# Mixing norm's root taken behind its projections, its squares summed during the down projection, and weight splits put in front of the roots of three stages

## The chip, the cores and the metric

The kernel runs on one core of one Trainium2 chip. The metric is the device time of one execution in microseconds (us). The kernel before takes 2094.03 us (median of three executions, 2090.93 to 2095.31).

## What is computed

Two transformer blocks run one after the other over 512 tokens of width 1024 in fp32. The change touches the second block, whose sequence has 16 meta tokens in front (528 tokens). Of it this matters:

```python
def rmsnorm(x, g):
    y = xf * lax.rsqrt(jnp.mean(xf * xf, axis=-1, keepdims=True) + EPS)
    return y * g
h = h + 0.5 * swiglu(rmsnorm(h, ffn1_norm), w_gate, w_up, w_down)      # stages up2, down2
u = rmsnorm(h, mix_norm)                                              # the mixing norm
(aq, ak, av, gq, gk, gv, gr, g_low, gate_a, gate_b) = split(u @ w_in) # stage back
ya = window_sink_attention(aq, ak, av, sinks)
log_a = log_sigmoid(g_low @ gla_gate_w + gla_gate_b) / 16
og = gated_linear_attention(gq, gk, gv, log_a)
yb = rmsnorm(og, gla_out_norm) * silu(gr)
mixed = sigmoid(gate_a) * (ya @ w_branch_att) + sigmoid(gate_b) * (yb @ w_branch_gla)  # merge2
h = h + mixed @ w_out                                                 # out2
h = h + 0.5 * swiglu(rmsnorm(h, ffn2_norm), ...)                      # up3, down3
```

The root of a token is one number that multiplies the whole row of `u`. So `u @ w_in` equals `(h * g) @ w_in` times that number, and the factor can be put on the product.

## The kernel before

Activations lie with features on the 128 partitions: eight tiles `k` of 128 features by 528 tokens. Each fp32 operand of a projection is split into a high and a low part (`H_hi`/`H_lo`, `W_hi`/`W_lo`, `G_hi`/`G_lo`), and TensorE forms hi·hi, lo·hi and hi·lo, three matmuls for each pair of tiles. Weights come in chunks of 128x2048 (`WC`; down projections 128x1408; the first chunk of `back`, "low", 128x1024). There are two buffers of each kind. SyncE loads chunk c into `W_raw` when chunk c-2 is split; ScalarE's `split` copies it to `W_hi` when TensorE has used chunk c-2; VectorE's `split` makes `W_lo` from both; TensorE then uses the chunk. ScalarE, VectorE and TensorE each run their instructions strictly in the order of the code, so what stands ahead of a `split` there delays it. The matmuls of a chunk have two groups of PSUM banks in turn (`psum_free0`, `psum_free1`), and a group is used again when an engine has evicted it.

The stages that matter come in this order: `up2` (22 chunks), `down2` (16 chunks, two for each feature tile of the residual `X`), `back` (14 chunks), `merge2` (8), `out2` (4), `up3` (22), `down3`.

- The norms ahead of `up2` and `up3` (`RMS_1`, `RMS_2`) are "late": TensorE starts with `H = x * gain`, and inside the second chunk it sums the squares over the partitions (`late_root`, in `project_late`). ScalarE takes the square root, VectorE the reciprocal into `RS`, and VectorE multiplies each product by `RS` as it evicts it (line 2089). `walk(..., after_first=...)` sets the order on ScalarE and VectorE: split of the second chunk, root, eviction of the first chunk, split of the third chunk.
- The mixing norm (`RMS_MIX`) is a plain one. After the last tile of `down2`, TensorE sums eight squared tiles (`statistic`), ScalarE takes the root, VectorE the reciprocal `INV`, then for each tile VectorE scales, ScalarE rounds to `H_hi`, and VectorE makes `H_lo`. The chunk "low" of `back` follows the tiles one by one, and the split of the next chunk stands behind all of them.
- `back` begins with four chunks in a row: "low" (16 columns, which go into the small gate matmuls), two of queries, one of keys and values. Then `win_steps` (35 steps of the windowed attention, each with some six projection matmul groups between) and `gla_steps` (30 steps of the gated linear attention) are woven with the remaining ten chunks. ScalarE and VectorE run the same steps in the same order. Products are evicted by ScalarE in the main (`back_low`, `back_query`, `back_key_value`, `back_value`, `back_gate`).

## Time and profile before

| | |
|---|---|
| median of three executions | 2094.03 us (2090.93 to 2095.31) |
| profiled execution, its own time | 2093.15 us |
| its span, from first to last instruction | 2091.3 us |
| TensorE (PE) busy | 1983.7 us, 95% |
| VectorE (DVE) busy | 1005.7 us, 48% |
| ScalarE (ACT) busy | 727.0 us, 35% |
| mean granted TensorE clock | 0.983 of full speed |

TensorE is the engine that is nearly always at work; a time to its left in the rows further down is in us from the start of the span. "PE PS L600" is any matmul (line 600 is the helper that issues them), "DVE W_lo L1625" is VectorE's split, "ACT ... L1184" any operation of ScalarE.

### The profile page before, as it was taken

What the parts mean: (1) busy time and instruction counts of PE and PEld (TensorE: products, weight loads), DVE (VectorE), ACT (ScalarE), POOL (GpSimd) and SP (SyncE); (2) the same over time, 40 slices, a digit from 0 to 9 for tenths busy, and PEclk for the clock granted to TensorE, in tenths of its full rate; (3) what the DMA queues carried; (4) which work ended last, traced back from release to release, by engine and by line L of the source; (5) the groups of instructions that cost most, each with busy time, mean ns of one, the idle gap of its engine ahead of it and who ended that gap; (6) DMA issues with size and microseconds to landing.
All of it is one profiled execution on the core that took longest, in us unless ns stands there. A gap on an engine that the chain in (4) does not pass through costs nothing.

```text
span 2091.3 us, 26797 instructions
## 1 busy us (share of the span) xinstructions
PE 1983.7 (95%) x10909; PEld 1671.3 (80%) x10909; DVE 1005.7 (48%) x1364; ACT 727.0 (35%) x972; POOL 23.8 (1%) x45
## 2 busy tenths in 40 slices
PE   5899999997999999979999999899999999999997
PEld 2787887873888888769999999687888878888885
DVE  7688753436455542264443322667323454444323
ACT  2454444324445532152222212455333332222111
POOL 0100000000000000000000000000000000000000
PEclk9999999998999999999999999999999999999999
DMA  6644212220222222212222222211112222222221
GB/s 269 215 158 134 99 61 102 102 99 20 81 97 83 100 83 97 102 39 82 100 80 94 72 95 92 73 61 42 61 61 81 102 81 99 100 100 74 97 90 61
DMA packets 34847, 195.45 MB, mean 93 GB/s; under 512 B 3680, under 2 KB 3696, under 8 KB 19552
## 3 DMA queue, kind: packets, MB, share of 16 engines
q1 hardware_dynamic: 29008, 173.55, 23.6%
q0 software_dynamic: 5776, 21.02, 3.1%
q8 instruction: 44, 0.72, 0.1%
q14 instruction: 19, 0.16, 0.0%
HBM read 192.46 MB, written 2.10 MB: 93 GB/s over the span
## 4 chain that ended last, share of the span: by engine, by line
PE 88%; DVE 8%; ACT 2%; issue 1%; DMA 1%; SPq 0%; DVEq 0%; ACTq 0%
PE PS L600 86%; DVE W_lo L1625 2%; DVE INV L1669 1%; DMA A_low<-in_wada 1%; PE PS L756 1%; ACT W_hi L1184 1%; DVE N L1674 1%; DVE A_high L2103 1%; DMA ring<-in_wada 0%; DVE ring L2103 0%; DVE RS L1646 0%; DVE PT_lo L1707 0%; DVE stats L1692 0%; DVE X L2135 0%; DVE stats L1856 0%
## 5 line engine op out<-in xcount | busy, mean ns | idle before, releaser
L600 PE MATMUL PS<-H_hi,W_hi 128*128 128x512 f32 (+1 forms) x1976 | 632.2, 354 | 48.8 <-DVE H_lo L1657 19.4
L600 PE MATMUL PS<-H_hi,W_lo 128*128 128x512 f32 (+1 forms) x1976 | 632.9, 354 | 0.0
L600 PE MATMUL PS<-H_lo,W_hi 128*128 128x512 f32 (+1 forms) x1976 | 632.0, 354 | 0.0
L1625 DVE TENSOR_TENSOR W_lo<-W_raw,W_hi 128x2048 fp32r<-128x2048 f32 (+2 forms) x170 | 352.9, 2076 | 311.6 <-ACT W_hi L1184 311.0
L600 PEld LDWEIGHTS PS<-H_hi,W_hi 128*128 128x128 f32 x1976 | 350.0, 191 | 106.6 <-issue 42.8
L1184 ACT ACTIVATE W_hi<-W_raw 128x2048 fp32r<-128x2048 f32 (+2 forms) x170 | 295.6, 1739 | 325.4 <-PE PS L600 324.6
L600 PEld LDWEIGHTS PS<-H_lo,W_hi 128*128 128x128 f32 x1976 | 349.3, 191 | 50.6 <-issue 0.2
L600 PEld LDWEIGHTS PS<-H_hi,W_lo 128*128 128x128 f32 x1976 | 349.1, 191 | 49.9 <-issue 0.2
L600 PE MATMUL PS<-G_hi,W_lo 128*128 128x512 f32 (+1 forms) x704 | 210.2, 339 | 0.0
L600 PE MATMUL PS<-G_hi,W_hi 128*128 128x512 f32 (+1 forms) x704 | 209.6, 338 | 0.0
L600 PE MATMUL PS<-G_lo,W_hi 128*128 128x512 f32 (+1 forms) x704 | 209.3, 338 | 0.0
L2089 DVE TENSOR_TENSOR T<-PS,RS 128x528 f32<-128x528 f32 (+1 forms) x88 | 57.4, 694 | 174.5 <-PE PS L600 174.4
L600 PEld LDWEIGHTS PS<-G_lo,W_hi 128*128 128x128 f32 x704 | 120.6, 188 | 15.7
L600 PEld LDWEIGHTS PS<-G_hi,W_hi 128*128 128x128 f32 x704 | 120.6, 188 | 15.2 <-issue 0.4
L600 PEld LDWEIGHTS PS<-G_hi,W_lo 128*128 128x128 f32 x704 | 120.4, 188 | 15.3
L1184 ACT ACTIVATE G_hi<-T 128x1024 f32 (+3 forms) x33 | 35.3, 1070 | 231.8 <-DVE T L2095 210.7
L2061 DVE SCALAR_TENSOR_TENSOR T<-PS,V,T 128x511 f32<-128x511 f32 (+1 forms) x88 | 60.0, 744 | 111.4 <-ACT T L1184 111.4
L1184 ACT ACTIVATE T<-T 128x1024 f32<-128x1024 f32 (+1 forms) x34 | 36.4, 1070 | 155.5 <-DVE T L2089 154.5
L1184 ACT ACT_TABLE_LOAD x45 | 57.7, 1283 | 51.5 <-PE PS L600 50.2
L1184 ACT ACTIVATE PT_hi<-PS 128x128 fp32r<-128x128 f32 (+3 forms) x64 | 27.9, 437 | 100.2 <-PE PS L756 100.2
L600 PE MATMUL PS<-W_lo,H_hi 128*128 128x256 f32 x208 | 62.0, 298 | 0.0
L600 PE MATMUL PS<-W_hi,H_hi 128*128 128x256 f32 x208 | 59.4, 286 | 2.1 <-DVE W_lo L1625 2.1
(246 smaller groups left out, 2045.2 us busy)
## 6 DMA issues: line engine op xcount, KB each, us to landing
W_raw<-in_wts SPq DMA_DIRECT2D x119, 1024.0 KB, 4.8
W_raw<-in_wdown SPq DMA_DIRECT2D x48, 704.0 KB, 4.1
ring<-in_wada POOLq DMA_DIRECT2D x32, 512.0 KB, 3.8
A_high<-in_wada SPq DMA_DIRECT2D x6, 1024.0 KB, 18.0
A_low<-in_wada SPq DMA_DIRECT2D x2, 1024.0 KB, 10.5
X<-in_xT SPq DMA_DIRECT2D x2, 1024.0 KB, 10.0
X<-in_xT POOLq DMA_DIRECT2D x1, 2048.0 KB, 8.8
out<-N SPq DMA_DIRECT2D x8, 256.0 KB, 2.1
```

The lines of the kernel that those rows point to most:

```text
L600: return nc.tensor.matmul(*a, **kw)
L756: last = nc.tensor.transpose(PS[:, TURNED, j * P:(j + 1) * P], PR[:, u % 3, j * P:(j + 1) * P], ident)
L1184: return nc.scalar.activation(*a, **kw)
L1625: vector.tensor_tensor(W_lo[:, c.odd, 0:size], W_raw[:, c.odd, 0:size], W_hi[:, c.odd, 0:size].bitcast(FP32), ALU.subtract).then_inc(w_lo, 1)
L1669: vector.reciprocal(INV[:, 0:n.tok], DEV[:, 0:n.tok]).then_inc(n.sem("inverse"), 1)
L1674: vector.scalar_tensor_tensor(out=N2[:, k, 0:n.tok], in0=n.centred(k), scalar=n.gain(k), in1=INV[:, 0:n.tok], op0=ALU.mult, op1=ALU.mult). ...
L2061: ins = vector.scalar_tensor_tensor(out=tile[:, m, tap:SEQ], in0=PS[:, 4 * b.odd + 2 * m, 0:SEQ - tap], scalar=w, in1=tile[:, m, tap:SEQ], ...
L2089: ins = vector.tensor_tensor(halves((TA, TB)[k][:, m, 0:tok], tok), pview(b, m, tok), halves(RS[:, 0:tok], tok), ALU.mult)
L2103: vector.scalar_tensor_tensor(out=w, in0=w, scalar=1.0, in1=silu_c[:, :], op0=ALU.mult, op1=ALU.mult, accum_out=mod[:, t:t + 1]).then_inc( ...
```

## The change

Five things are done; the rest of the diff is what they need (buffers, semaphores).

1. `down2` is written out tile by tile on ScalarE and VectorE. As soon as a residual tile is there, ScalarE makes `H_hi = x * gain` and the square, and VectorE makes `H_lo` and adds the square to a running sum in `TA`. The split of `back`'s second chunk (the first queries) stands right behind the last tile.
2. TensorE starts "low" without a norm, and sums `TA` over the partitions inside the first query chunk, after three of its eight tiles (`late_root`). The small gate matmuls behind that chunk wait for ScalarE's root. 16 matmuls of statistics go, 2 come.
3. All products of `back` are multiplied by the root. VectorE does it as it evicts low, queries, keys and values, the `gr` and gate chunks (before, ScalarE evicted these). The factors of the linear attention's q and k are multiplied by `RS` in three operations at attention steps 3 to 5 (`back_factor`). For the token-major values TensorE turns `RS` into a column of 5 numbers for each partition (5 matmuls of one column), VectorE copies it (`RSC`), and ScalarE scales with it, in four operations in place of two. In `merge2` VectorE multiplies the gate product and ScalarE then takes its sigmoid from SBUF.
4. In `up2` and `up3` (and in `back` on ScalarE) the split of the third chunk stands ahead of the root on ScalarE, and ahead of the reciprocal on VectorE.
5. In `up3` TensorE sums the squares after two tiles of the second chunk, not after six.

```diff
-                chunks_of_round(0, 0, s.words[0])
+                split(At(s.c + 1), s.words[0])
+                after_first()
+                for k in range(per):
+                    body(0, 0, k)
...
-            pool.wait_ge(*RMS_MIX.reach("scaled", 1))
+            pool.wait_ge(w_used, st["back"].c)
+            pool.wait_ge(sem("hidden_lo"), 2 * FH)
...
+                        n = 6 if tok == TOK else 2
+                        feature_tile(outs_of(b, m, tok, at), c.odd, 0, tiles * P, range(n), act_hi, act_lo, stop=False)
                         within_first()
-                        feature_tile(outs_of(b, m, tok, at), c.odd, 6 * tiles * P, tiles * P, range(6, KT), act_hi, act_lo, start=False)
+                        feature_tile(outs_of(b, m, tok, at), c.odd, n * tiles * P, tiles * P, range(n, KT), act_hi, act_lo, start=False)
...
+            def late_root(n):
+                pe.wait_ge(*n.reach("added", n.sums))
+                total = TA if n is RMS_MIX else N1
+                for o, (t0, tn) in n.outs(n.late_bank):
+                    last = mm(o, inv_d[:, :], total[:, 0, t0:t0 + tn], start=True, stop=True)
...
+                        for n in range(NB + 1):
+                            t0 = META + n * P if n < NB else 0
+                            mm(PS[:, TURNED, 2 * P + n:2 * P + n + 1], RS[:, t0:t0 + P], ident[:, 0:1], start=True, stop=True)
...
+                            if k == 1 and m == 0 and kt == 3:
+                                late_root(RMS_MIX)
...
+                        pe.wait_ge(*RMS_MIX.reach("deviation", 1))
...
-            norm(RMS_MIX, st["back"].held)
...
+            def square_of(k):
+                n = RMS_MIX
+                wait_src(act, n, k)
+                if k == 0:
+                    act.wait_ge(sem("hidden_prod"), HIDDEN["up2"] + FH + 1)
+                if k >= 4:
+                    act.wait_ge(*n.reach("added", k - 3))
+                activate(square_tile(k), n.src(k), ACT.Square).then_inc(n.sem("squared"), 1)
...
+            def back_query(g):
+                act.wait_ge(sem("att_q_raw"), g + 1)
+                activate(WQH[:, 2 * g:2 * g + 2, :], GR[:, 2 * g:2 * g + 2, :], ACT.Copy, scale=QSCALE).then_inc(sem("att_q_hi"), 1)
...
+            def back_key():
+                act.wait_ge(sem("att_k_raw"), 1)
                 for at, tok, n in KEY_PIECES:
-                    ins = activate(KWH[:, at:at + n], PS[:, back_bank(b, tok // HALF), tok % HALF:tok % HALF + n], ACT.Copy)
+                    ins = activate(KWH[:, at:at + n], KT_flat[:, tok:tok + n], ACT.Copy)
...
-                for m in range(2):
-                    ins = activate(LV[:, 2 * m:2 * m + 2, col:col + 256], PS[:, bank + m, :].rearrange("p (b n) -> p b n", b=2), ACT.Copy)
+                for blk in range(NB):
+                    ins = activate(LV[:, blk, col:col + 256], PS[:, bank + blk // 2, blk % 2 * 256:blk % 2 * 256 + 256], ACT.Copy,
+                                   scale=RSC[:, blk:blk + 1])
...
                 split(At(s.c + 2), words[s.c + 2])
+                late_root(RMS_MIX)
                 back_logit()
-                back_query(s, 1)
+                back_query(0)
...
+                    split(At(s.c + 2), WC)
...
-            only_split("down2", 4, 4)
-            norm(RMS_MIX)
+            s = st["down2"]
+            for f in range(KT):
+                for half in range(2):
+                    split(At(s.c + 2 * f + half + 1), words[s.c + 2 * f + half + 1])
+                    if f and half == 0:
+                        late_tile(RMS_MIX, f - 1)
+                        square_of(f - 1)
+            late_tile(RMS_MIX, KT - 1)
+            split(At(st["back"].c + 1), WC)
+            square_of(KT - 1)
...
+            def add_square(k):
+                n = RMS_MIX
+                dve.wait_ge(*n.reach("squared", k + 1))
+                if k >= 2:
+                    dve.wait_ge(*n.reach("added", k - 1))
+                vector.tensor_tensor(square_tile(0), square_tile(0), square_tile(k), ALU.add).then_inc(n.sem("added"), 1)
+            def mix_root():
+                n = RMS_MIX
+                add_square(KT - 1)
+                dve.wait_ge(*n.reach("deviation", 1))
+                vector.reciprocal(RS[:, :], RS[:, :]).then_inc(n.sem("inverse"), 1)
                 dve.wait_ge(*n.reach("inverse", 1))
...
+            def back_low(s):
+                used(At(s.c))
+                retire(vector.tensor_tensor(halves(TC[0:RANK, 0, :], TOK), PS[0:RANK, 0:2, 0:HALF], halves(RS[0:RANK, :], TOK), ALU.mult),
+                       s, At(0))
+            def scaled_pair(s, k, dst, done):
+                used(At(s.c + k))
+                b, g = BATCH_OF[k], BACK[k][1]
+                bank = back_bank(b, 0)
+                vector.tensor_tensor(dst[:, 2 * g:2 * g + 2, :], PS[:, bank:bank + 2, :], root_twice(), ALU.mult).then_inc(sem(done), 1)
+            def freed(k, done, value):
+                dve.wait_ge(sem(done), value)
+                dve.sem_inc(psum_free[BATCH_OF[k] % 2], 1)
...
+                dve.wait_ge(sem("back_part"), PART_OF[k])
+                vector.tensor_tensor(halves(KT_flat, TOK), back_halves(b), halves(RS[:, :], TOK), ALU.mult).then_inc(sem("att_k_raw"), 1)
+                freed(k, "att_k_raw", 1)
+                used(At(s.c + k))
+                vector.tensor_tensor(halves(VT[:, :], TOK), back_halves(b + 1), halves(RS[:, :], TOK), ALU.mult).then_inc(sem("att_v"), 1)
+                dve.wait_ge(sem("att_v"), 1)
+                dve.sem_inc(psum_free[(b + 1) % 2], 1)
                 dve.wait_ge(sem("att_k_hi"), 1)
                 for at, tok, n in KEY_PIECES:
-                    ins = vector.tensor_tensor(KWL[:, at:at + n], PS[:, back_bank(b, tok // HALF), tok % HALF:tok % HALF + n],
...
+            def back_factor(n):
+                dve.wait_ge(sem("decays"), 1)
+                to, of = ((TA, LE), (TB, TB), (LL, LL))[n]
+                vector.tensor_tensor(to[:, :, :], of[:, :, :], root_all(), ALU.mult).then_inc(sem("factors"), 1)
...
+                    if 3 <= t < 6:
+                        back_factor(t - 3)
...
+                    if k > BACK_FIRST_GLA:
+                        scaled_gate(s, k - 1)
+                yield GLA_STEPS
+                scaled_gate(s, len(BACK) - 1)
+            def scaled_gate(s, k):
+                what, g, _ = BACK[k]
+                dst, done = (GR, "gr_raw") if what == "gr" else (GB, "gate_kept")
+                scaled_pair(s, k, dst, done)
+                freed(k, done, g + 1)
...
             def back(s):
-                split(At(s.c + 1), words[s.c + 1])
+                mix_root()
+                back_low(s)
                 split(At(s.c + 2), words[s.c + 2])
+                scaled_pair(s, 1, GR, "att_q_raw")
+                freed(1, "att_q_raw", 1)
                 back_abs()
-                back_query(s, 1)
+                back_query(0)
                 split(At(s.c + 3), words[s.c + 3])
                 back_sums()
-                back_query(s, 2)
+                scaled_pair(s, 2, GR, "att_q_raw")
+                freed(2, "att_q_raw", 2)
+                back_query(1)
...
+                        if name == "merge2":
+                            used(c)
+                            for m in range(2):
+                                ins = vector.tensor_tensor(TB[:, m, 0:SEQ], PS[:, 4 * b.odd + 2 * m, :], RS[:, META:TOK], ALU.mult)
+                            retire(ins, s, b)
...
+                walk(dve, split, s, FH, 2, body, lambda: late_root(n, lambda: split(At(s.c + 2), WC)))
...
-            residual_sum("down2", 1, 0.5, TOK, 0)
-            norm(RMS_MIX)
+            s = st["down2"]
+            for f in range(KT):
+                b = At(f)
+                for half in range(2):
+                    split(At(s.c + 2 * f + half + 1), words[s.c + 2 * f + half + 1])
+                used(At(s.c + 2 * f + 1))
+                x = halves(X[:, f, :], TOK)
+                vector.scalar_tensor_tensor(out=x, in0=pview(b, 0, TOK), scalar=0.5, in1=x, op0=ALU.mult, op1=ALU.add
+                                            ).then_inc(sem("residual"), 1)
+                dve.wait_ge(sem("residual"), RESIDUAL["down2"] + f + 1)
+                dve.sem_inc(psum_free[f % 2], 1)
+                late_tile(RMS_MIX, f)
+                if f >= 2:
+                    add_square(f - 1)
+            split(At(st["back"].c + 1), WC)
```

How the instructions stand is seen at three places.

VectorE around the root of `up2`, before (`N1` or `N` are the squares, `T` the evicted product, `W_lo` a split):

```order
L1643 TENSOR_TENSOR N<-N 128x1056 x3
L1643 TENSOR_TENSOR N<-N 128x528
L1646 RECIPROCAL RS<-RS 128x528
L2089 TENSOR_TENSOR T<-PS,RS 128x528 x2
L1625 TENSOR_TENSOR W_lo<-W_raw,W_hi 128x2048
L2089 TENSOR_TENSOR T<-PS,RS 128x528 x2
```

The same place in the changed kernel:

```order
L1683 TENSOR_TENSOR N<-N 128x528
L1665 TENSOR_TENSOR W_lo<-W_raw,W_hi 128x2048
L1687 RECIPROCAL RS<-RS 128x528
L2193 TENSOR_TENSOR T<-PS,RS 128x528 x4
L2199 TENSOR_TENSOR T<-T 128x1056
```

The split of the third chunk has moved from behind the reciprocal and the first eviction to ahead of both. `up3` shows the same with 128x512.

VectorE from the last down split to the splits of `back`, before (`X` the residual, `INV` and `N` the norm, the 128x1024 split is "low"):

```order
L1625 TENSOR_TENSOR W_lo<-W_raw,W_hi 128x1024
L2036 SCALAR_TENSOR_TENSOR X<-PS,X 128x528
L1669 RECIPROCAL INV<-DEV 128x528
L1674 SCALAR_TENSOR_TENSOR N<-X,V,INV 128x528 x2
L1655 TENSOR_TENSOR H_lo<-N,H_hi 128x528
...
L1655 TENSOR_TENSOR H_lo<-N,H_hi 128x528 x2
L1625 TENSOR_TENSOR W_lo<-W_raw,W_hi 128x2048 x2
```

The same place in the changed kernel (`T<-T` adds a square to the sum, `T<-PS,RS 16x528` evicts "low", `GR` takes the first queries):

```order
L1665 TENSOR_TENSOR W_lo<-W_raw,W_hi 128x1024
L2318 SCALAR_TENSOR_TENSOR X<-PS,X 128x528
L1673 SCALAR_TENSOR_TENSOR H_lo<-X,V,H_hi 128x528
L1695 TENSOR_TENSOR T<-T 128x528
L1665 TENSOR_TENSOR W_lo<-W_raw,W_hi 128x2048
L1695 TENSOR_TENSOR T<-T 128x528
L1701 RECIPROCAL RS<-RS 128x528
L1835 TENSOR_TENSOR T<-PS,RS 16x528
L1665 TENSOR_TENSOR W_lo<-W_raw,W_hi 128x2048
L1843 TENSOR_TENSOR GR<-PS,RS 128x1024
```

The reciprocal now stands behind the split of the first query chunk and ahead of the split of the second; sixteen operations of the norm (scale and low part of eight tiles) have gone from between.

VectorE in the attention's steps 2 to 4 in the changed kernel (`stats` and `PRW` are the softmax of one unit, `PTW_lo` and `PTM_lo` the low part of its turned probabilities):

```order
L1665 TENSOR_TENSOR W_lo<-W_raw,W_hi 128x2048
L1885 TENSOR_TENSOR T<-LE,RS 128x1056
L1939 TENSOR_REDUCE stats<-PS 128x1
L1942 TENSOR_SCALAR stats<-stats,V 128x1
L1949 TENSOR_TENSOR stats<-stats 128x1
L1952 RECIPROCAL stats<-stats 128x1
L1954 TENSOR_SCALAR PRW<-PRW,stats 128x272
L1962 TENSOR_TENSOR PTW_lo<-PS,PTW_hi 128x128
L1964 TENSOR_TENSOR PTM_lo<-PS,PTM_hi 16x128
L1885 TENSOR_TENSOR T<-T,RS 128x1056
```

The two rows with `RS` are new, and a third (`LL<-LL,RS`) follows one step later; without them the rows are those of before.

## Rows read from the trace of the kernel before

**Rows 1.** Page: busy us by engine; one group: xcount | busy us, mean ns | idle

```profile
PE 1983.7 (95%) x10909; PEld 1671.3 (80%) x10909; DVE 1005.7 (48%) x1364; ACT 727.0 (35%) x972; POOL 23.8 (1%) x45
...
L2089 DVE TENSOR_TENSOR T<-PS,RS 128x528 f32<-128x528 f32 (+1 forms) x88 | 57.4, 694 | 174.5 <-PE PS L600 174.4
```

**Rows 2.** Waits of PE over the span: total us, times, longest us

```profile
PE PS L600 <- DVE W_lo L1625: 12.0, 4, 3.8
PE PS L600 <- DVE H_lo L1655: 7.5, 4, 6.6
```

**Rows 3.** Timeline, end of down2 and start of back: start, us, what [idle before]

```profile
1301.24 0.41 PE L600 MATMUL PS<-G_hi,W_lo 128*128 128x264 f32 x2
...
1302.56 7.36 PE L600 MATMUL PS<-SQ,inv_d 128*128 128x264 f32 x32 [0.91 <-issue]
...
1303.09 1.28 ACT L1184 ACT_TABLE_LOAD   x1
...
1316.51 0.78 PE L600 MATMUL PS<-H_hi,W_hi 128*128 128x264 f32 x2 [6.59 <-DVE H_lo L1655]
...
1324.11 1.90 ACT L1184 ACTIVATE W_hi<-W_raw 128x2048 fp32r<-128x2048 f32 x1
...
1328.39 0.50 PE L600 MATMUL PS<-H_hi,W_hi 128*128 128x512 f32 x1 [2.39 <-DVE W_lo L1625]
```

**Rows 4.** Timeline, first query chunk's end to the attention's first steps

```profile
1339.72 2.04 PE L600 MATMUL PS<-T 16*128 16x264 f32 x8
...
1346.29 2.29 DVE L1625 TENSOR_TENSOR W_lo<-W_raw,W_hi 128x2048 fp32r<-128x2048 f32 x1
...
1350.74 1.26 DVE L1815 TENSOR_TENSOR T<-T 128x1056 f32<-128x1056 f32 x1 [2.16 <-ACT T L1184]
...
1355.86 1.22 DVE L1781 SCALAR_TENSOR_TENSOR WQL<-PS,WQH 128x1024 fp32r<-128x1024 f32 x1
...
1361.18 1.06 DVE L1791 TENSOR_TENSOR KWL<-PS,KWH 128x264 fp32r<-128x264 f32 x6 [1.66 <-ACT KWH L1184]
...
1375.12 0.40 PE L600 MATMUL PS<-KWH,WQH 64*128 64x272 f32 x2 [1.44 <-ACT PRW L1184]
...
1376.02 0.44 DVE L1856 TENSOR_REDUCE stats<-PS 128x1 f32<-128x272 f32 x1 [0.52 <-PE PS L600]
```

**Rows 5.** Timeline of PE, the linear attention's first turns and its end

```profile
1472.48 1.28 PE L894 MATMUL PS<-CF,LL 128*128 128x128 f32 x10
...
1565.05 0.49 PE L600 MATMUL PS<-H_hi,W_hi 128*128 128x512 f32 x1 [1.39 <-ACT GB L1184]
```

**Rows 6.** Timeline, root of up2 and of up3

```profile
925.01 1.05 PE L600 MATMUL PS<-N,inv_d 128*128 128x264 f32 x4
925.71 0.60 PE L600 MATMUL PS<-H_hi,W_hi 128*128 128x264 f32 x2
...
926.84 3.45 DVE L1646 RECIPROCAL RS<-RS 128x528 f32<-128x528 f32 x1 [2.69 <-ACT RS L1184]
...
937.03 0.51 PE L600 MATMUL PS<-H_hi,W_hi 128*128 128x264 f32 x2 [3.66 <-DVE W_lo L1625]
...
1712.11 1.02 PE L600 MATMUL PS<-N,inv_d 128*128 128x512 f32 x2
...
1723.91 0.79 PE L600 MATMUL PS<-H_hi,W_hi 128*128 128x512 f32 x1 [3.82 <-DVE W_lo L1625]
```

**Rows 7.** Windows: span, length, busy us (instructions) by engine, granted clock, DMA share, GB/s

```profile
937.00:942.00 5.00, 4.97 (x28) 4.98 (x29) 3.64 (x4) 2.55 (x2) 0.00 (x0) 0.66 0.60 211
1326.00:1330.00 4.00, 1.61 (x8) 1.34 (x8) 3.82 (x2) 2.41 (x3) 0.00 (x0) 1.00 0.20 37
1365.00:1463.00 98.00, 88.92 (x708) 78.02 (x707) 71.12 (x243) 51.51 (x182) 0.00 (x0) 0.98 0.13 44
1419.00:1422.00 3.00, 3.00 (x17) 2.50 (x17) 2.16 (x6) 0.39 (x3) 0.00 (x0) 0.52 0.24 44
1724.00:1730.00 6.00, 6.00 (x15) 4.70 (x16) 4.27 (x5) 2.86 (x2) 0.00 (x0) 0.52 0.49 175
```

More of the change, by code:

```diff
@@ L190, in build_program @@
         one = sb("one", [P, 1], FP32)
+        RSC = sb("RSC", [P, NB + 1], FP32)
         small = sb("small", [P, 3, GLA_HEADS * NB], FP32)
@@ L1088, in merge_one @@
                         last.then_inc(w_used, 1)
-            def late_root(n):
-                pe.wait_ge(*n.reach("added", 4))
-                for o, (t0, tn) in n.outs(n.late_bank):
-                    last = mm(o, inv_d[:, :], N1[:, 0, t0:t0 + tn], start=True, stop=True)
-                last.then_inc(n.sem("variance"), 1)
             def project_late(name, n, norm_of, tok, at):
```

110 lines of the change are left out of this document (53 added, 57 removed).

## The prediction

> **What bounds the kernel now.** I read the page's busy times first: TensorE is busy for 1983.7 us of the span, VectorE for less than half [rows 1]. So time is won only where TensorE stops or runs at a lower clock. The waits of TensorE say for whom it stops: 12.0 us for splits, with the longest 3.8 us, and 7.5 us for the low parts that the mixing norm makes [rows 2]. The timeline then shows what lies around three of these stops, and the windows the clock behind them.
>
> - *End of `down2`.* The last down matmul pair is issued at 1301.24. A query chunk's 48 matmuls of 512 columns take 11.33 us (1328.39 to 1339.72), 0.236 us each, so a pair of 264 columns takes 0.243, and the next chunk could start at 1301.49. The first query chunk really starts at 1328.39 [rows 3, 4]. In these 26.9 us TensorE does statistics (7.36 us), waits 6.59 us for the first normed tile, does "low" at the pace of the norm, and waits 2.39 us for the split [rows 3].
> - *Roots of `up2` and `up3`.* TensorE waits 3.66 and 3.82 us for the split of the third chunk, which on both other engines stands behind root, reciprocal and first eviction [rows 6]. Behind each wait the granted clock falls to its lower level, 1.2 GHz: its mean is 0.66 over the 5 us from 937, and 0.52 over the 6 us from 1724 [rows 7]. Behind the wait of 2.39 us at 1328.39 it stays at 1.00, which is 2.4 GHz [rows 3, 7].
>
> **What the parts of the change cost and give.** All is reckoned against the profiled execution's own 2093.15 us, which is 0.9 us under the median of the runs; its span is 2091.3 us, and the 1.8 us around it stay.
>
> *The gap behind `down2`.* What remains of the 26.9 us is "low": 24 pairs at 0.243 us, 5.9 us with the start. It may run at once, since seven of eight tiles are made during `down2`, and the last comes in time: three operations on 528 columns (residual, `H_hi`, `H_lo`) at some 0.7 us, the mean of that size [rows 1], from 1301.7 to 1304.0, and TensorE gets to it at about 1306.7. The split of the query chunk: `W_hi` 1.90 us behind `H_hi` (1303.2 to 1305.1), `W_lo` 2.29 us, so 1307.4, just as "low" ends [rows 3, 4]. TensorE then starts queries at 1307.45 in place of 1328.39. **Gain 20.9 us.** In `down2` each engine gets two such operations more per tile. A chunk there is 33 pairs, 8.0 us of TensorE; a split behind residual, tile and sum is done 5 us into it (0.7 of 2048 columns' 1.90 and 2.29 for the split, and 2.1), so they cost nothing. Without that cover they would cost 1.4 us a tile, 11 in all.
>
> *The root in the query chunk.* Two matmuls of sums delay TensorE by 0.7 us (925.01 to 925.71 is the same) [rows 6]. **Cost 0.7 us.** The chunk's matmuls take 11.3 us, so it ends at 1319.45. ScalarE: `W_hi` of the next chunk from 1307.5 to 1309.4, table load 1.28, root 0.7, so 1311.4. VectorE: reciprocal 3.45, low 0.6, split 2.29, so 1317.8 [rows 1, 3, 4, 6]. TensorE wants this split only after the gate matmuls, 2.04 us [rows 4], at 1321.5. Margin 3.7 us, no wait.
>
> *Up to the attention.* Query chunk two runs to 1332.8. VectorE evicts the first queries (1.22 us, by the row for 1024 columns from PSUM), and the rest goes as before; the split for the key chunk is ready at 1328.4 [rows 4]. The gate sums on VectorE take 5.1 us (1350.74 to 1355.86) from 1330.6 to 1335.8, then queries two 1.2 us; the value half needs that group only at 1338.7. But what follows is late: low part of the queries, the split (2.29, to 1342.3), keys times root (0.7, to 1343.0) [rows 1, 4]. ScalarE's decays end at 1344.3, then the key's high part 0.8; TensorE has finished the value half at 1344.5. VectorE still has values times root (0.7) and the key's low part (1.06 for six pieces, 0.9 for five) [rows 4], so 1346.1. Before, that part was done in the middle of the chunk. Queued behind it are the first scores, and with them all of TensorE. **Cost 1.7 us**, between nothing (if the chain runs ahead) and 2.2.
>
> *In the attention.* Five one-column matmuls are ten passes; ten turns of 128 columns take 1.28 us at most [rows 5]. **Cost 1.1 us.** Three products with `RS` of 1056 columns cost VectorE 1.26 us each [rows 4], the copy of `RSC` 0.2. They stand ahead of the row maximum, for which ScalarE's exponential and TensorE's next scores wait. There TensorE already stops 1.44 us on this chain, so the first counts in full, while VectorE was idle 0.52 us before the next maximum [rows 4] and I give the third about as much. **Cost 2.8 us**, bounds 0 (all in idle time) and 4.0 (all on the path). Scaling the values in four operations instead of two lengthens ScalarE's step twice by some tenths. No row shows the 256-column form; it costs between nothing and one wait like 1.44 us, and I take 0.3.
>
> *Behind it.* Gate evictions move from ScalarE to VectorE, 1.2 us in place of 1.0; only the last is waited for, as now with 1.39 us [rows 5]. **Cost 0.2 us.** In `merge2` the product comes 11 us ahead of its use: nothing. Without that cover 1.3 us for each of four.
>
> *`up2` and `up3`.* The split of the third chunk fits between the sums and the root: in `up2` VectorE's sums end before TensorE takes them, at 925.01, in fact at 924.2; ScalarE has nothing between the first chunk's end and the root, and `W_lo` is done at 926.5; the reciprocal starts at 926.84 as it does now [rows 6]. TensorE's second chunk ends at 933.4, when the first is long evicted. In `up3` the sums come 2.8 us earlier (1709.3), which makes room: the split ends at 1712.3, the reciprocal follows to 1715.7, the eviction to 1717, and TensorE is there at 1720. Both stops go, with the clock that they cost: 5 x 0.34 = 1.7 us and 6 x 0.48 = 2.9 us [rows 7]. **Gains 3.7 + 1.7 and 3.8 + 2.9 us**, 12.1 in all.
>
> Sum: 20.9 + 12.1 - 0.7 - 1.7 - 1.1 - 2.8 - 0.3 - 0.2 = 26.2 us, so 2093.15 - 26.2 = **2067.0 us**, 1.3% faster.
>
> **The rivals.**
>
> - *The root comes too late (a new wait in the place of the old).* The chain root, reciprocal, low, split is serial, and the margin of 3.7 us is my reckoning. If it slips by more, TensorE stops ahead of the second query chunk, and with a stop as long as those of `up2` the clock falls behind it: 3.7 + 1.7, so 2072.4. Against it: each link has a row. Chance 0.13.
> - *The attention hides it all.* VectorE is busy 71.1 of 98 us there [rows 7]. If the factors and the key chain fall into its idle time, the costs 1.7 and 2.8 go: 2062.5. Against it: TensorE already waits in these steps. Chance 0.15.
> - *The clock falls once more.* The stop ahead of the first scores and those of the next steps lie close together. One fall like that behind `up2` or `up3` adds 1.7 to 2.9 us: 2069.5. Chance 0.12.
> - *The stops of `up2` and `up3` only move* to the next chunk, if its PSUM group is still taken: 12.1 us are not won, 2079. Against it: eviction ends 1.7 and 3 us before need. Chance 0.06.
> - *Slower: the attention at the low clock.* There TensorE does small groups between waits. At 1419 the clock fell to 0.52 for some 3 us although TensorE was at work [rows 7]. If the added stops keep it at 1.2 GHz, each us at that level loses about 0.48 us (from the 6 us at 0.52). The gain of 26.2 us is used up when 55 of the 98 us run so; over the whole stage the loss is 47 us and more, and the time 2115. The Trainium skill ("TensorE: Matmul & The Clock Gate", section "A second HAM failure mode: psum-queue depth-cycling") speaks for this: TensorE that idles briefly but often between matmul groups has its clock go down and up again, and throughput suffers. By that rule, the trace agrees only in part: this stage already has such idle moments and its mean clock is 0.98. Chance 0.04.
>
> **How the numbers follow.** My own forecast holds 0.50, the rivals the rest. From 2062 to 2074.5 lie my forecast with its bounds (-4.5 if the attention hides all, +1.2 and +0.5 for factors and keys at their upper ends, +1.2 for the values), most of the second rival, the first and the third: about 0.83. Within 0.2% (4.2 us, about what a measurement of this kernel can tell from no change) would take a loss of 22 us out of the sum: 0.02. Slower 0.04, faster 0.94.
>
> **What the profile of the changed kernel would show.** Right: no matmul on `SQ` at the end of `down2`, "low" at once and at full clock, its last pair followed by the queries within 0.5 us; no stop of TensorE over 1 us at either third chunk of `up2` and `up3`, and clock 1.00 behind; a stop of 1 to 2.5 us ahead of the first scores, released by `KWL`; TensorE's idle time in the attention up by about 3 us. Wrong: a wait for `W_lo` ahead of the second query chunk; a wait for an eviction (`T<-PS,RS`) in `up2` or `up3`; splits of `down2` that TensorE waits for; a mean clock under 0.95 in the attention.

## The result, and the profile after

The changed kernel takes 2077.76 us (median of four executions, 2077.51 to 2079.00) against 2093.36 us before beside it (median of four; 2090.93 to 2095.31); the ratio is 0.9928, with a 95% interval of 0.9914 to 0.9941. It is faster, by 15.6 us where 26.2 were forecast, and lies outside the forecast range of 2062 to 2074.5 us. The profiled execution of after took 2077.65 us, with a span of 2075.8 us.

The first lines of the page of after, which answer to [rows 1] (share of the span and instructions behind each busy time):

```profile
span 2075.8 us, 26753 instructions
PE 1982.6 (96%) x10891; PEld 1667.3 (80%) x10891; DVE 1025.1 (49%) x1385; ACT 723.9 (35%) x965; POOL 23.8 (1%) x45
```

The waits of TensorE of after (total us, times, longest), which answer to [rows 2]:

```profile
PE PS L621 <- ACT PRW L1212: 4.0, 2, 2.6
PE PS L913 <- DVE PTM_lo L1964: 2.5, 3, 2.1
PE PS L621 <- DVE PTM_lo L1964: 2.5, 4, 0.9
PE PS L621 <- DVE W_lo L1665: 2.1, 1, 2.1
PE PS L621 <- DVEq L1847: 1.6, 1, 1.6
```

Of the 12.0 us for `W_lo` one wait of 2.1 us in the first block is left, and the 7.5 us for `H_lo` of the mixing norm are gone. `ACT PRW`, the probabilities that the next scores wait for, rose to 4.0 from this row of before:

```profile
PE PS L600 <- ACT PRW L1184: 2.8, 2, 1.4
```

The timeline of after behind `down2` answers to [rows 3]. The row with `G` is the last pair of `down2`; the first row of TensorE (PE) with 128x512 is the first of the queries:

```profile
1300.32 0.41 PE L621 MATMUL PS<-G_hi,W_lo 128*128 128x264 f32 x2
1300.77 0.71 DVE L2318 SCALAR_TENSOR_TENSOR X<-PS,X 128x528 f32<-128x528 f32 x1 [5.65 <-PE PS L621]
1301.51 0.74 ACT L1212 ACTIVATE H_hi<-X,V 128x528 fp32r<-128x528 f32 x1 [7.65 <-DVE X L2318]
1302.16 1.90 ACT L1212 ACTIVATE W_hi<-W_raw 128x2048 fp32r<-128x2048 f32 x1
1304.09 2.29 DVE L1665 TENSOR_TENSOR W_lo<-W_raw,W_hi 128x2048 fp32r<-128x2048 f32 x1 [0.42 <-ACT W_hi L1212]
1306.44 0.50 PE L621 MATMUL PS<-H_hi,W_hi 128*128 128x512 f32 x1
1308.63 1.05 PE L621 MATMUL PS<-T,inv_d 128*128 128x264 f32 x4
1310.66 3.45 DVE L1701 RECIPROCAL RS<-RS 128x528 f32<-128x528 f32 x1 [3.66 <-ACT RS L1212]
1318.66 2.04 PE L621 MATMUL PS<-T 16*128 16x264 f32 x8
1320.63 0.50 PE L621 MATMUL PS<-H_hi,W_hi 128*128 128x512 f32 x1
```

From the last matmul pair of `down2` to the first query matmul it is 6.12 us, where it was 27.15: a gain of 21.03. No row of TensorE here has a wait in brackets, at the second query chunk (1320.63) neither.

The windows of after (the columns are busy us and instructions of PE, PEld, DVE, ACT and POOL, then the granted clock), for `up2` behind its third chunk, and for `up3`, which answer to [rows 7]:

```profile
930.00:948.00 18.00, 18.00 (x150) 18.00 (x149) 10.90 (x8) 5.98 (x5) 0.00 (x0) 1.00 0.24 80
1700.00:1725.00 25.00, 25.00 (x108) 20.08 (x107) 14.17 (x11) 9.72 (x9) 0.00 (x0) 1.00 0.24 85
```

TensorE is busy without a gap and at 2.4 GHz: both stops are gone, with the low clock behind them [rows 6, 7].

The attention of after, with the new costs in it. The scores (`KWH,WQH`) stop TensorE for 2.01 us, and a factor product (`T<-LE,RS`, 1.24 us) stands ahead of the chain on which the next scores wait for 2.62 us, with its brackets `<-ACT PRW`:

```profile
1345.76 0.34 PE L621 MATMUL PS<-KWH,WQH 64*128 64x144 f32 x2 [2.01 <-issue]
1352.72 0.40 PE L621 MATMUL PS<-KWH,WQH 64*128 64x272 f32 x2 [0.35 <-DVE RSC L1877]
1357.42 1.24 DVE L1885 TENSOR_TENSOR T<-LE,RS 128x1056 f32<-128x1056 f32 x1
1359.93 0.59 PE L621 MATMUL PS<-KWH,WQH 64*128 64x272 f32 x2 [2.62 <-ACT PRW L1212]
```

So where are the missing us? The first and last start of the matmuls on one tile give the length of each stretch. The table has them in us, worked out from those starts in each trace (experiments beside it):

| stretch | before | after | e1 | e4 | e5 | e10 | e13 |
|---|---|---|---|---|---|---|---|
| merge1 (first matmul on O to first on M) | 77.0 | 78.2 | 77.0 | 77.0 | 76.2 | 76.3 | 76.3 |
| out1 (M, first to last) | 43.3 | 44.6 | 43.2 | 43.2 | 43.3 | 43.3 | 43.3 |
| norms and up1, to first on G | 295.2 | 294.9 | 294.0 | 295.2 | 290.0 | 289.7 | 289.4 |
| down1 (G) | 122.1 | 122.8 | 122.2 | 122.1 | 123.1 | 120.0 | 119.9 |
| norm and up2 | 291.0 | 286.7 | 285.5 | 284.2 | 284.6 | 284.4 | 284.4 |
| down2 | 127.8 | 128.3 | 127.8 | 127.8 | 127.8 | 127.8 | 127.8 |
| back, and merge2 to first on O2A | 274.9 | 263.8 | 262.5 | 274.9 | 264.5 | 267.9 | 261.5 |
| merge2, to first on M2 | 77.0 | 78.1 | 77.0 | 77.0 | 77.0 | 77.0 | 76.9 |
| out2 (M2) | 43.2 | 44.6 | 43.2 | 43.2 | 43.2 | 43.3 | 43.3 |
| up3 | 252.6 | 245.7 | 245.8 | 245.8 | 240.5 | 240.5 | 240.5 |
| down3 | 121.8 | 122.6 | 121.9 | 121.9 | 120.7 | 119.4 | 119.5 |

Stages in which TensorE has the same work as before got longer: merge1 by 1.2 us, out1 by 1.3, down1, down2 and down3 by 0.5 to 0.8, merge2 by 1.1, out2 by 1.4, which is 7.0 us in all. The change rewrote `down2` and the evictions of `merge2` on the other two engines, but it left the first block alone, and each matmul takes longer there too. What changed in all of them is the place of the buffers: `CB` (512 bytes in each partition) went into an overlay and `RSC` took 32 bytes, so what is allocated behind `RSC`, among it O, M and G, lies 480 bytes lower. The weights `W_hi` and `W_lo` and the activations H are allocated ahead of both and stayed.

### The profile page after: what moved, and what is told of

It is laid out like the page before. It is cut to its first block, busy times and chain, and to the rows that moved or that the text cites. A ratio compares the mean times of both kernels' runs of the same rounds, so it can differ in the third digit from the quotient of the medians.

```text
span 2075.8 us, 26753 instructions
## 1 busy us (share of the span) xinstructions
PE 1982.6 (96%) x10891; PEld 1667.3 (80%) x10891; DVE 1025.1 (49%) x1385; ACT 723.9 (35%) x965; POOL 23.8 (1%) x45
## 4 chain that ended last, share of the span: by engine, by line
PE 89%; DVE 7%; ACT 1%; issue 1%; DMA 1%; SPq 0%; DVEq 0%; ACTq 0%
PE PS L621 88%; DVE W_lo L1665 1%; DMA A_low<-in_wada 1%; PE PS L778 1%; DVE INV L1724 1%; DVE A_high L2207 1%; DMA ring<-in_wada 0%; DVE ring L2207 0%; ACT W_hi L1212 0%; DVE N L1729 0%; DVE PT_lo L1762 0%; DVE stats L1747 0%; DVE X L2239 0%; DVE stats L1939 0%; DVE PTW_lo L1962 0%
## 5 line engine op out<-in xcount | busy, mean ns | idle before, releaser
L1212 ACT ACTIVATE T<-T 128x1024 f32<-128x1024 f32 (+1 forms) x38 | 40.6, 1069 | 171.6 <-DVE T L2193 149.4
```

What stands on the lines that cost most here:

```text
L1212: return nc.scalar.activation(*a, **kw)
```

## The experiments

**The place of the buffers (e1, e2, e3) and the roots alone (e4).** e1 is the changed kernel with

```diff
-        one = sb("one", [P, 1], FP32)
-        RSC = sb("RSC", [P, NB + 1], FP32)
+        ones = sb("ones", [P, 1 + NB + 1], FP32)
+        one, RSC = ones[:, 0:1], ones[:, 1:NB + 2]
```

e2 is the kernel before with `sb("pad", [P, 8], FP32)` ahead of `mod`; e3 the kernel before with `CB` in its overlay and `sb("pad", [P, 16], FP32)` in its old place; e4 the kernel before with parts 4 and 5 of the change, in `up2` and `up3` alone.

> The changed kernel, with RSC put into the 32 bytes that `one` has in each partition anyway, so that every buffer behind it lies at a multiple of 128 bytes again where it did before (512 bytes lower), not 32 bytes past one. Theory A (the address): in the changed kernel the matmuls of 512 columns that read M, O, O2A and O2G take 395 ns in place of 389 (0.2333 us from one to the next in out2 in place of 0.2267), 768 of them, 5.1 us, and the 1056 wide ones on G about 1 ns each more. So here 389 ns again, the part up to up2 shorter by 2.8 us, merge2 and out2 by 2.5, the time 2077.8 - 5.5 = 2072 us. Rival B (the cadence differs from run to run, or comes from VectorE's traffic in merge2): 395 ns stays, 2077.8 us.

> The kernel before, with nothing but an unused buffer of 32 bytes per partition ahead of `mod`, so that all that lies behind it starts 32 bytes later. Theory A (the address): M, O, O2A, O2G at 395 ns, 5 to 6 us slower than before, 2099 us, half of it ahead of up2. Rival B (the cadence has nothing to do with the address): no change, 2093.4 us.

> The kernel before, with CB in its overlay (as in the changed kernel) and an unused buffer of 64 bytes in its place: all that lies behind starts 448 bytes lower, at 64 bytes past a multiple of 128. It tells what alignment counts. Theory A1 (multiples of 64 bytes are enough): 389 ns, no change, 2093.4 us. Theory A2 (multiples of 128 are needed): 395 ns or more for M, O, O2A, O2G, 5 us slower, 2098.5 us. What speaks for A2: G's tiles are 2112 bytes apart and so lie at 0 and 64 past a multiple of 128 in turn, and their wide matmuls take 393 ns in the kernel before. Rival B (not the address): 2093.4.

> The kernel before, with the parts 4 and 5 of the change alone (split of the third chunk ahead of root and reciprocal in up2 and up3, sums after two tiles in up3); no address changes. By the prediction 12.1 us less, 2081.3 us. By what the trace of after shows (up2 and down2 together 3.8 us shorter where 5.4 were reckoned, merge2 to the final norm 3.6 where 6.7 were reckoned less 0.2, of which the address would explain 2.5): 9.8 us, 2083.6 us. Rival (the stops only move, or the clock falls elsewhere): 2088 us or more.

Measured, beside the kernel before (2093.43 us); four or five executions each, ten of e3: e1 2068.78 us (ratio 0.9886, 0.9870 to 0.9901); e2 2103.18 (1.0054, 1.0040 to 1.0068); e3 2097.68 (1.0018, 1.0009 to 1.0028); e4 2081.86 (0.9943, 0.9930 to 0.9957). The matmuls on M, one row of each trace (shortest, median and longest ns), in the order before, after, e1, e2, e3:

```profile
L600 PE MATMUL PS<-M_hi,W_hi x128: 389/389/389, 422.0 to 1696.1; 128*128 128x512 f32 x128
```
```profile
L621 PE MATMUL PS<-M_hi,W_hi x128: 393/395/397, 423.1 to 1686.4; 128*128 128x512 f32 x128
```
```profile
L621 PE MATMUL PS<-M_hi,W_hi x128: 389/389/389, 423.0 to 1678.0; 128*128 128x512 f32 x128
```
```profile
L601 PE MATMUL PS<-M_hi,W_hi x128: 393/395/397, 421.4 to 1704.8; 128*128 128x512 f32 x128
```
```profile
L601 PE MATMUL PS<-M_hi,W_hi x128: 397/397/398, 422.6 to 1702.7; 128*128 128x512 f32 x128
```

An unused pad of 32 bytes alone makes the kernel before 9.7 us slower; 32 bytes taken back make the changed kernel 9.0 us faster. Theory A stands, B falls. e3 shows that a multiple of 64 bytes isn't enough (A2). In e2 the stages named above account for 6.9 us, and between after and e1 they account for 6.9 us too. The rest of e2 lies in `up2` (2.1) and `back` (2.6), less `up3` (-1.1), and the first two go with the clock: H didn't move, and e2's trace has a mean granted clock of 0.97 in `up2` and 0.97 in the 270 us behind `down2`, where that of before has 0.98 in both (for `back` see the table of steps further down). So 7 us are shown to come from the address. Whether the other 2 to 3 us of e1 and e2 have to do with it isn't shown.

**What the distance must be (e5, e9, e10).** e5 views H and G as dense tiles wherever 512 tokens are used:

```diff
+        def dense_view(t, n):
+            return t[:, :, :].rearrange("p k t -> p (k t)")[:, 0:n * SEQ].rearrange("p (k t) -> p k t", t=SEQ)
+        HC_hi, HC_lo = dense_view(H_hi, KT), dense_view(H_lo, KT)
+        def g_of(tok):
+            return (G_hi, G_lo) if tok == TOK else (dense_view(G_hi, FT), dense_view(G_lo, FT))
```

> The changed kernel with RSC beside `one` (as in e1_aligned, 2068.8 us), and besides: where only 512 of the 528 tokens are used (all of the first block, up3, down1, down3), the tiles of H and G lie 2048 bytes apart and begin at a multiple of 128 bytes; till now they are 2112 apart, so every second one lies 64 bytes past a multiple. Theory A (the address of the moving operand costs): some 2900 matmuls of 512 columns on H and 1056 on G get faster; at half of the 8 ns that M lost between 0 and 64 bytes past (389 to 397 ns in e3_moved_64) that is 4 ns x 3960 = 16 us, 2053 us, and G goes from 393 to 389 ns. Rival B (it counts for M, O and O2 only, through what else runs there): no change, 2068.8 us.

> e1_aligned, and behind the final norm's sums 26 groups of 48 matmuls of 128x128 (24 to a PSUM bank; the last three groups 264 columns wide), ahead of them one group of 120. Their results are used nowhere. Stationary operand: four blocks of W_lo in turn; moving: W_hi, both at 128 bytes past a multiple of 512. The moving operand is shifted by 0, 16, 32, 64, 96, 128, 192, 224, 256, 288, 320, 384 and 448 bytes; then the stationary one by 32, 64, 128, 256 and 384; then both together by 64, 128 and 256; then every third moving operand alone by 384 and by 64. Theory A1 (64 bytes): 0.2267 us from one to the next at 0, 64, 128 ..., 0.2333 at 16, 32, 96, 224, 288. Theory A3 (512 bytes, or the distance between the two operands): 0.2267 at shift 0 alone; if it is the distance, also where both are shifted. e3_moved_64 speaks against A1 (M at 64 bytes past: 0.2333). Rival B (what else runs beside TensorE sets it): all groups alike.

> e5_dense (2057.1 us), with the dense tiles of G_lo begun 128 bytes later, so that they too lie at 128 bytes past a multiple of 512, as G_hi, H, M, O and the weights do. In e5_dense down1 took 123.1 us and down3 120.7 (122.2 and 121.9 in e1_aligned), and G_lo (at a multiple of 512) was the slower operand. Theory A3 (all operands at the same place in 512 bytes are fast): 0.2267 us per matmul in both, 528 of them, 119.7 us each, 2057.1 - 3.4 - 1.0 = 2052.7 us. Theory A1 (128 bytes are enough): no change, 2057.1 us.

e5 took 2057.14 us (0.9827, 0.9813 to 0.9841), 11.6 less than e1 where some 16 were expected, and e10 2054.34 (0.9812, 0.9798 to 0.9825), 2.8 less than e5 where 4.4 were expected. In the traces the two down stages did lose 4.4 us from e5 to e10; `back`, which they have in common, was 3.4 us longer in e10's. Against e1 the stretch of `up1` won 4.0 us and that of `up3` 5.3, but down1 got slower by 0.9. The probe tells why. Four of its 26 groups, from the trace of e9 (L1214: no shift; L1229: moving operand shifted by 128 bytes; L1238: by 256; L1271: both operands by 128):

```profile
L1214 PE MATMUL PS<-W_hi,W_lo x48: 389/389/389, 2085.0 to 2095.7; 128*128 128x512 f32 x48
L1229 PE MATMUL PS<-W_hi,W_lo x48: 392/394/398, 2140.4 to 2151.4; 128*128 128x512 f32 x48
L1238 PE MATMUL PS<-W_hi,W_lo x48: 389/389/397, 2174.0 to 2184.7; 128*128 128x512 f32 x48
L1271 PE MATMUL PS<-W_hi,W_lo x48: 387/389/398, 2296.0 to 2306.7; 128*128 128x512 f32 x48
```

From a group's first start to that of the next it is 10.9 us at no shift and at 256 bytes, 11.0 at 64 and 320, 11.1 at 16, and 11.2 at 32, 96, 128, 192, 224, 288, 384 and 448. Shifting the stationary operand alone does the same (11.2 us at 32, 64, 128 and 384, 10.9 at 256), and shifting both together costs nothing (10.9 at 64, 128 and 256). With every third moving operand alone off it is 11.0 at 384 bytes and 11.1 at 64. So neither A1 nor A3 was right as written: it is the distance between the two operands that counts, and it should be a multiple of 256 bytes. The other engines were idle by then, so rival B falls for good. The probe was executed once, and it doesn't repeat the kernel at 64 bytes: there a shift by 64 costs a third of one by 32 (11.0 and 11.2 us), while in e3, with M 64 bytes off, out2 takes the same 44.6 us as with M 32 bytes off (e2). So the multiple of 256 is shown, and what a given other distance costs is not settled. In e5 `G_lo` was 128 bytes off such a multiple. With that mended (e10), all wide matmuls on G take 389 ns:

```profile
L632 PE MATMUL PS<-G_hi,W_hi 128*128 128x512 f32 x352 | 137.0, 389 | 0.2 <-DVE G_lo L2196 0.2
L632 PE MATMUL PS<-G_hi,W_lo 128*128 128x512 f32 x352 | 136.9, 389 | 0.0
L632 PE MATMUL PS<-G_lo,W_hi 128*128 128x512 f32 x352 | 136.9, 389 | 0.0
```

and down1 and down3 fall to 120.0 and 119.4 us (expected 119.7). In e5 the trace leaves one thing unexplained: down3 ran faster than down1 with the same addresses.

**The terms of the attention (e6, e7, e8, e12), each against e1 (2068.78 us, 0.9886).** e6 leaves out the three calls of `back_factor`; e8 leaves out the five matmuls on `RS`, `RSC` and the `scale=`; e12 moves those matmuls ahead of the first scores; e7:

```diff
 # ScalarE
-                back_decays()
                 back_key()
+                back_decays()
 # VectorE
+                back_key(3)               # keys times RS, ahead of the split
                 split(At(s.c + 4), words[s.c + 4])
                 back_key_value(s, 3)      # KWL, and only then values times RS
```

> e1_aligned without the three products of back_factor: the linear attention's q and k are left without the root (this part of the computation is left out). The prediction counted 2.8 us for them: 2066.0 us. Theory C (they set off further stops or a fall of the clock, and so make up the missing us of the attention): 4 us or more, 2064.8 or less. Rival D (they lie in VectorE's idle time): 2068.8 us, no change.

> e1_aligned with the keys ahead in both queues: VectorE multiplies the keys ahead of the split of the fifth chunk and makes KWL ahead of the values; ScalarE makes KWH ahead of the decays. The prediction counted 1.7 us for the stop ahead of the first scores (2.01 us in the trace). If it goes and nothing takes its place: 2066.8 us. Theory C (the stop also sets off later ones and a lower clock): 2065.5 or less. Rival D (the stop goes, but the values or the decays are then late by as much): 2068.8 us.

> e1_aligned without the turned root: no matmuls of one column, no RSC, the token-major values are evicted unscaled in two operations in place of four (this scaling is left out). The prediction counted 1.1 us for the matmuls and 0.3 for the evictions: 2067.4 us. Theory C (they delay the chain of the scores and cost more): 2066 or less. Rival D (hidden): 2068.8 us.

> e1_aligned, with the five matmuls that turn the root put into TensorE's stop ahead of the first scores (2.01 us; they take 1.17). Leaving them and the scaled evictions out won 3.1 us (e8_no_turn, 2065.7), where the prediction counted 1.4. If the matmuls themselves cost (1.17 us and what they push back on the chain of the scores): 2067 us or less, down to 2066. Rival (the four evictions in place of two cost): 2068.8 us, no change.

Measured: e6 2064.55 us (0.9857, 0.9842 to 0.9872), 4.2 less than e1; e7 2067.26 (0.9868, 0.9853 to 0.9883), 1.5 less; e8 2065.72 (0.9866, 0.9851 to 0.9881), 3.1 less; e12 2066.41 (0.9866, 0.9851 to 0.9881), 2.4 less. These differences are small against what surrounds them. The intervals of all four touch that of e1, and e1 wasn't run beside them: by the ratios the same four differences are 6.1, 3.8, 4.2 and 4.2 us. So the traces have to tell what a term costs in its place.

Every second step of the attention starts with a group of scores on TensorE. The table has the time in us from the last matmul pair of `down2` to the first scores, and then the length of some of the stretches from one group of scores to the next, numbered from 1 to 15; those left out agree within 0.3 us. A star marks a stretch with a mean granted clock under 0.85 of full speed.

| stretch | before | e2 | after | e1 | e6 | e7 | e8 | e12 | e10 | e13 | e14 |
|---|---|---|---|---|---|---|---|---|---|---|---|
| to the first scores | 63.5 | 63.5 | 45.4 | 45.4 | 45.5 | 43.3 | 45.5 | 45.5 | 45.4 | 45.5 | 44.4 |
| 1 | 4.3 | 4.3 | 7.0* | 5.5 | 5.5 | 5.5 | 4.3 | 4.4 | 8.3* | 5.7* | 4.4 |
| 2 | 6.0 | 6.0 | 7.2 | 7.2 | 6.0 | 7.2 | 7.2 | 7.2 | 7.7* | 7.2 | 7.2 |
| 3 | 6.9 | 6.9 | 8.5* | 8.5* | 6.9 | 8.4* | 8.4* | 8.4* | 8.4 | 7.4 | 8.4* |
| 4 | 4.8 | 4.8 | 4.8 | 4.8 | 4.8 | 4.8 | 4.8 | 4.8 | 6.0* | 4.8 | 4.8 |
| 6 | 4.5 | 5.8* | 4.5 | 4.5 | 4.5 | 5.8* | 4.5 | 5.8* | 5.8* | 4.5 | 5.8* |
| 8 | 4.8 | 6.0* | 6.0* | 6.0* | 6.0* | 6.0* | 4.8 | 6.0* | 6.0* | 6.0* | 6.0* |
| 10 | 5.5* | 5.7* | 5.7* | 4.5 | 5.7* | 5.7* | 5.5* | 5.7* | 5.7* | 5.7* | 5.7* |
| 15 | 9.3 | 9.3 | 9.3 | 10.8* | 9.3 | 9.3 | 9.3 | 9.3 | 9.3 | 9.3 | 9.3 |

At equal clock the terms can be read off:

- *Keys (e7).* The first scores come 2.1 us sooner than in e1.
- *One-column matmuls (e8, e12).* Stretch 1 is 1.1 us shorter without them. With them in the stop, it is 1.05 us shorter, and the first scores come no later: the stop fell from 2.0 us to the row below. The copy of `RSC` and what goes with it is the 0.07 us between 4.33 us (e8) and 4.40 us (e12).
- *Factors (e6).* Stretch 2, with one product in it, is 1.2 us shorter without; stretch 3, with two, 1.5 us (8.4 at full clock in e10, 6.9 in e6). With only one product in it (e13) it is 7.4.
- *The clock.* From stretch 4 on the traces differ by 1.0 to 1.5 us at a time, and the star goes with the longer time, not the edit: stretch 8 takes 4.8 us in before and 6.0 in e2, which have the same attention. In stretch 3 the low clock costs nothing (8.4 us in e10 without it). e1 has three starred stretches, e6 and e8 two, e7 and e12 four. That is why the times don't measure the terms: of the 3.1 us of e8, 1.1 are the matmuls, and a starred stretch less is about as much again.

```profile
PE PS L621 <- DVE KWL L1866: 1.0, 1, 1.0
```

**GpSimd for the factors (e11).**

```diff
+            pool.wait_ge(sem("decays"), 1)
+            for to, of in ((TA, LE), (TB, TB), (LL, LL)):
+                nc.gpsimd.tensor_tensor(to[:, :, :], of[:, :, :], root_all(), ALU.mult).then_inc(sem("factors"), 1)
```

> e1_aligned, with the three products of back_factor made by GpSimd, which does nothing else in the attention. Without them the time was 2064.6 us (e6_no_factors) against 2068.8. If GpSimd runs beside VectorE and is ready before the q's of the linear attention are evicted: 2064.6 us. Rival D1 (GpSimd and VectorE hold each other up at SBUF): 2067 or more. Rival D2 (GpSimd is too slow, the eviction of gq and with it TensorE waits): 2070 or more.

Measured 2071.05 us (0.9894, 0.9879 to 0.9909). By its time that is D1 or D2, and the trace decides for D1: no wait for the eviction of gq turned up, and the loss lies ahead of the first scores:

```profile
1337.74 2.41 POOL L618 TENSOR_TENSOR T<-LE,RS 128x1056 f32<-128x1056 f32 x1 [40.82 <-ACT LE L1215]
1338.08 0.71 DVE L1864 TENSOR_TENSOR VT<-PS,RS 128x528 f32<-128x528 f32 x1 [1.90 <-PE PS L624]
1338.94 6.50 DVE L1869 TENSOR_TENSOR KWL<-LV,KWH 128x272 fp32r<-128x272 f32 x5
1342.67 2.54 POOL L618 TENSOR_TENSOR LL<-LL,RS 128x1056 f32<-128x1056 f32 x1
```

VectorE's five small operations for `KWL`, 1.01 us in after, take 6.50 us while GpSimd multiplies, and TensorE's stop ahead of the scores grows from 2.0 to 7.5 us (its longest wait in e11):

```profile
PE PS L624 <- issue: 7.5, 1, 7.5
```

What e6 won is more than lost there. The Trainium skill ("SBUF — State Buffer", section "SBUF: two separate sides") says that a VectorE operation with two inputs in SBUF and a GpSimd operation that reads SBUF exclude each other, each for its whole length. The trace agrees as far as it goes: the operations with two inputs in SBUF took 6.50 us for 1.01, while `VT<-PS,RS`, with one input in PSUM, took its 0.71 us beside GpSimd; how long a single operation was held no row shows.

**Both together, on the dense tiles (e13, e14).** e13 is e10 with the turn of e12 and k's factor product made in VectorE's idle 1.9 us ahead of the values; e14 is e10 with the orders of e7 and e12.

> e10_dense_g (0.9812 of the time before), with the turned root ahead of the first scores (as in e12_turn_ahead, which won 2.4 us) and one of the three factor products (k's) put where VectorE waits 1.91 us for the values, ahead of the first scores. If the stops in the attention are what costs there: 2.4 us for the turn and 1.0 (a third of the 3.1 us that e6_no_factors won) for the product, 3.4 us under e10_dense_g, ratio 0.9796. Rival (the granted clock sets the attention's time and falls from run to run in other places, whatever the stops): no more than 1 us under e10_dense_g, ratio 0.9807 or more.

> e10_dense_g with the keys ahead in both queues (as in e7_keys_first, which won 1.5 us) and the turned root ahead of the first scores. No stop is left to hide its 1.17 us, but it no longer stands on the way from the first scores to the second. If both add up: 2.5 to 3 us under e10_dense_g, ratio 0.9799. Rival (the clock): no more than 1 us, 0.9807 or more.

Measured: e13 2047.99 us (0.9788, 0.9772 to 0.9804), e14 2047.98 (0.9781, 0.9768 to 0.9794): 2.1 and 2.2% faster than the kernel before, 1.4% faster than the changed one, and some 6 us under e10, where 3.4 and 3 were expected. The rival had put the time too high, but in the traces its mechanism, the clock, goes with most of what came on top. Windows of 270 us from the end of `down2` on (clock in the third column from the right), of e1, e9, e10 and e13; up to the final norm e9 is the same program as e1, and e10 has the same attention as both:

```profile
1295.70:1565.70 270.00, 256.10 (x1682) 219.15 (x1681) 151.88 (x339) 112.11 (x249) 1.60 (x3) 0.98 0.18 62
```
```profile
1296.70:1566.70 270.00, 256.40 (x1672) 219.78 (x1671) 150.24 (x339) 111.98 (x249) 1.61 (x3) 0.97 0.18 62
```
```profile
1283.60:1553.60 270.00, 256.15 (x1661) 220.62 (x1660) 149.58 (x338) 109.28 (x247) 1.60 (x3) 0.96 0.17 62
```
```profile
1283.60:1553.60 270.00, 257.10 (x1686) 220.17 (x1686) 151.99 (x339) 112.35 (x249) 1.61 (x3) 0.98 0.18 62
```

The same program gave 0.98 and 0.97 (0.981 and 0.969 by windows of 10 us), and the stretch of `back` 262.5 and 264.8 us; in e10 it gave 0.96 and 267.9. In e13 it is 261.5, only 1.0 less than in e1. So some 5 us of any single profile of this part come and go with the clock. Of the 6.4 us by which e13's `back` is shorter than e10's, its orders account for 2.0 by the table of steps (1.05 for the turn, 1.0 for the product); the rest is stretches that ran at the low clock in e10's trace. The mean clock of the whole program points the same way: 0.980 to 0.984 in the five executions of e10, 0.985 in four of the five of e13 and 0.982 in the slowest of them.

Chance alone it may not be. In stretch 1 the clock fell in four of the seven traces with a stop of 2.0 us ahead of the first scores (after, e5, e9 and e10; not in e1, e6 and e8), in e11 with 7.5 us, in one of two with 1.0 us (e13, not e12), and in none of the six without a stop there (before, e2, e3, e4, e7, e14). One trace of each kernel doesn't settle how often; how much of e13's and e14's extra 3 us the missing stops brought by way of the clock stays open.

## Why the prediction was wrong

Of the waits, overlaps and chains that the prediction names, nearly all came as told, and the sum had a hole: what the moved buffers cost every matmul that reads them. In medians: 2093.4 us, less 11.6 for parts 4 and 5 (e4), less 13.1 for parts 1 to 3 (e1 against e4), plus 9.0 for the place of the buffers (after against e1), is 2077.7. Such a chain of differences closes by itself; what it tells is that with the buffers put right (e1) the time is 2068.8, 1.8 us above the 2067.0 forecast and inside the range.

- *The step that failed.* "What the parts of the change cost and give" goes through instructions and waits only. No term, no bound and no rival speaks of the buffers that the change moves: the sum puts at nothing, without a reason, what that does to matmuls that are otherwise left alone. The stages with them took 7.0 us more. 768 wide matmuls on M, O, O2A and O2G went from 389 to 395 ns in the rows, and from one to the next from 0.2267 to 0.2333 us, which is 5.1 us; the down stages add 2.0, where the wide ones on G went from 393 to 394 ns. The time is 9.0 us above e1's; the 2 us between 7.0 and 9.0 aren't told apart from the clock. The profile of before gave a hint that I passed over: M at 389 ns, and H and G of the same shape at 400 and 393.
- *A second hole, smaller: the clock.* The sum has no term for a longer low clock, and only the third rival speaks of one fall. In the profiled execution `back` came out 3.0 us above its terms (274.9 - 20.9 + 6.8 = 260.8 forecast, 263.8 measured), with low clock in stretches 1 (1.5 us longer than in e1) and 8 (1.2 us longer than in before), and `up2` 1.1 us. Together with the 7.0 that is the miss of 10.7 us to within 0.5. The 7.0 us alone would have given 2074.0, just inside the range; and the 3.0 and 1.1 alone 2071.1.
- *The gap behind `down2`:* 20.9 forecast, 21.03 measured. *Root sums in the query chunk:* 0.7; the chunk went from 11.33 to 12.22 us, so 0.9. *The root's chain:* in time, as reckoned; no wait ahead of the second query chunk.
- *`up2` and `up3`:* 5.4 and 6.7 forecast; the stretches shrank by 6.8 and 6.8 in e4, by 5.5 and 6.8 in e1. The rival that the stops only move is out. In medians e4 has 11.6 of the 12.1. That `up2` gained less in e1 is not part 4: behind the norm ahead of `up2` the low clock lasted longer than in e4. The windows of e1 and e4 at this place (clock in the third column from the right):

```profile
907.00:912.00 5.00, 4.72 (x21) 4.76 (x22) 5.00 (x9) 5.00 (x9) 0.00 (x0) 0.50 0.00 0
912.00:917.00 5.00, 5.00 (x39) 5.00 (x38) 3.49 (x5) 5.00 (x7) 0.00 (x0) 0.87 0.00 0
```
```profile
910.00:915.00 5.00, 4.79 (x28) 4.83 (x29) 5.00 (x9) 5.00 (x9) 0.00 (x0) 0.68 0.00 0
915.00:920.00 5.00, 5.00 (x43) 5.00 (x43) 3.48 (x5) 5.00 (x7) 0.00 (x0) 1.00 0.00 0
```

- *Keys ahead of the first scores:* 1.7 forecast, a stop of 2.01 us in the trace, 2.1 in place and 1.5 in time (e7).
- *One-column matmuls and scaled values:* 1.1 + 0.3 forecast, 1.1 in place (e8 against e1) and 3.1 in time. The price of the matmuls was right; in e8's trace the rest is one starred stretch less than in e1's. That four evictions in place of two cost anything is not shown.
- *Factors:* 2.8 forecast, 1.2 + 1.5 = 2.7 in place and 4.2 in time. The rival that the attention hides it all is out.
- *The last gate:* a wait of 1.6 us where it was 1.39, as forecast.
- *The clock falls once more* (the third rival) did happen, and more than once: between 1344 and 1380 of after the granted clock is 0.91, where before has 1.00 at the same steps up to 1410. Since it varies from run to run, it isn't a term of fixed size. The slower rival is out: the mean over the 270 us stayed at 0.97. The rule of the Trainium skill that the prediction quoted ("TensorE: Matmul & The Clock Gate", section "A second HAM failure mode: psum-queue depth-cycling") fits the falls between short stops, but not a loss of the size that the rival gave it.

## What to carry to other kernels

When a change adds, drops or moves a buffer, compare the mean duration of each shape of matmul, tile by tile, before reading any wait: if stages that weren't touched got slower, look at the distance between the operands. Keep that distance at a multiple of 256 bytes, by padding or by dense tiles: from after over e1 to e10 that gave 23 us, and the new orders of the attention (e13, e14) some 6 more, most of them with the clock. A term of 1 or 2 us can't be read from the time of a kernel whose clock falls at changing places: compare the same stretch of two traces, at the same granted clock.
